# A hybrid RG-LRU / gated delta net encoder: the turns of rg_loop cut at another place, the delta net's chunk matrices made in dn_project

## What is computed

```python
def rglru_mixer(y, w_in, conv_w, conv_b, gate_w, gate_b, lam, w_out):
    xb, zb = jnp.split(y @ w_in, 2, axis=-1)          # 1024 -> 2048 + 2048
    xb = dwconv(xb, conv_w) + conv_b                  # 4 taps along time
    for d in range(2):
        gates = einsum("btnc,gncm->gbtnm", xh, gate_w[d]) + gate_b[d]   # blocks of 256
        r, i = sigmoid(gates[0]), sigmoid(gates[1])
        log_a = -RG_C * softplus(-lam[d]) * r
        a = exp(log_a); b = sqrt(-expm1(2.0 * log_a)) * (i * xf)
        h_d = linear_recurrence(a, b)                 # d = 1 runs backwards
    return ((h_0 + h_1) * silu(zb)) @ w_out

# gated delta net, per direction, head and chunk
decay = exp(where(incl, gc[:, None] - gc[None, :], -inf))    # gc = cumsum(g)
a_mat = where(strict, einsum(kb, k) * decay, 0.0)            # kb = k * beta
sol = triangular_solve(a_mat + eye, [v * beta, kb * exp(gc)])
qk = einsum(q, k) * decay
# then the chunks of a head in a row: state s, outputs o
```

## Time and profile before

| | us |
|---|---|
| median of 3 runs | 3242.26 |
| lowest, highest | 3238.85, 3243.62 |
| the profiled execution | 3243.82 |
| its span | 3242.1 |
| PE busy | 2779.4 (86%) |
| DVE, ACT, POOL busy | 1628.7, 1224.1, 1253.5 |

### The profile page before, as it was taken

The page is one execution under the profiler, slowest core; times in us unless marked ns, Lnnn a source line. Parts: engine busy times, 40 slices in busy tenths (PEclk is TensorE's granted clock), DMA queues, the critical chain, the costliest instruction groups (busy, mean ns, idle before and its releaser), DMA issues. The chain is left out here.

```text
span 3242.1 us, 53074 instructions
## 1 busy us (share of the span) xinstructions
PE 2779.4 (86%) x19211; PEld 2661.3 (82%) x19211; DVE 1628.7 (50%) x2351; ACT 1224.1 (38%) x1989; POOL 1253.5 (39%) x1183
## 2 busy tenths in 40 slices
PE   4799999993997299999997998999989999995993
PEld 2788888883995199999996898888989889885992
DVE  3266666664202334444443776776767677663003
ACT  2255555553103134334433344534444453432001
POOL 3333333331220122222221766665666666642220
PEclk8899999996998599999998999998999899997996
DMA  3111111112314023332232312032131313114214
GB/s 108 53 52 52 52 52 52 52 39 87 111 65 171 19 72 90 94 93 88 85 91 69 92 18 74 17 78 51 40 77 17 74 17 76 28 17 145 79 39 170
DMA packets 187727, 223.34 MB, mean 69 GB/s; under 512 B 50715, under 2 KB 157548, under 8 KB 185884
## 3 DMA queue, kind: packets, MB, share of 16 engines
q1 hardware_dynamic: 182940, 203.98, 21.7%
q10 hardware_dynamic: 4608, 17.04, 1.6%
HBM read 152.77 MB, written 68.23 MB: 68 GB/s over the span
## 5 line engine op out<-in xcount | busy, mean ns | idle before, releaser
L1634 ACT ACTIVATE zz<-ps 104x416 fp32r<-104x416 f32 x560 | 284.9, 517 | 446.4 <-PE ps L1496 445.3
L537 PE MATMUL ps<-dn_yhi,dn_whi 128*128 128x416 f32 (+1 forms) x1152 | 387.1, 336 | 16.4 <-POOL dn_wlo L521 16.4
L538 PE MATMUL ps<-dn_ylo,dn_whi 128*128 128x416 f32 (+1 forms) x1152 | 376.1, 326 | 0.0
L539 PE MATMUL ps<-dn_yhi,dn_wlo 128*128 128x416 f32 (+1 forms) x1152 | 375.1, 326 | 0.0
L1726 DVE TENSOR_TENSOR pp<-ps,level_mask 104x416 fp32r<-104x416 f32 x560 | 318.8, 586 | 100.1 <-PE ps L1496 97.7
L1498 PE MATMUL ps<-pp,zz 104*104 104x208 f32 x1440 | 266.1, 295 | 41.4 <-ACT zz L1634 31.9
L537 PE MATMUL ps<-rg_yhi,rg_whi 128*128 128x416 f32 (+1 forms) x768 | 251.9, 328 | 45.8 <-POOL rg_wlo L521 40.4
L538 PE MATMUL ps<-rg_ylo,rg_whi 128*128 128x416 f32 (+1 forms) x768 | 251.6, 328 | 0.0
L539 PE MATMUL ps<-rg_yhi,rg_wlo 128*128 128x416 f32 (+1 forms) x768 | 250.6, 326 | 0.0
L1498 PE MATMUL ps<-zz,pp 104*104 104x208 f32 x1440 | 247.9, 282 | 0.0
L1498 PEld LDWEIGHTS ps<-pp,zz 104*104 104x104 f32 x1440 | 184.4, 176 | 67.2 <-ACT zz L1634 34.8
(11 more groups left out here) (275 smaller groups left out, 7476.8 us busy)
## 6 DMA issues: line engine op xcount, KB each, us to landing
dn_raw<-in_dn_w_in SPq DMA_DIRECT2D x48, 512.0 KB, 3.9
qd<-rows_scratch SPq DMA_DIRECT2D x160, 104.0 KB, 3.1
rg_raw<-in_rg_w_in SPq DMA_DIRECT2D x32, 512.0 KB, 3.8
o_scratch<-a SPq DMA_DIRECT2D x16, 520.0 KB, 2.8
rgo_oraw<-o_scratch ACTq DMA_DIRECT2D x16, 520.0 KB, 4.3
n_y<-y_scratch SPq DMA_DIRECT2D x16, 520.0 KB, 6.5
n_h<-h_scratch SPq DMA_DIRECT2D x16, 520.0 KB, 12.6
qk_scratch<-p_qk SPq DMA_DIRECT2D x16, 520.0 KB, 3.1
```

What stands on the lines that cost most here:

```text
L537: e.matmul(o, whi, mhi[:, t0:t0 + tn], start=(first and k == 0), stop=False)
L538: e.matmul(o, whi, mlo[:, t0:t0 + tn], start=False, stop=False)
L539: ins = e.matmul(o, wlo, mhi[:, t0:t0 + tn], start=False, stop=(last and k == end))
L1634: e.activation(zz[:, b, :, :], ps[0:CH, 2 * b + 1, 0:m4], ACT.Copy).then_inc(zev.sem, 1)
```

## The change

It has three parts, and a row of counters (`ahead`, `gone`) that let a phase start with loads for which no turn stands.

**rg_loop.** A turn n now makes units X0, X1 of block n + 1, then the gates of block n (direction 1 first), then Z0, Z1 of block n. X0 and X1 of block 0 stand ahead of the loop; the last turn has none. DVE's taps for block n + 1 stand between parts of block n.

```diff
+        xtile, tile = S("xtile", 2), S("tile", 10, 3)
         gate_hi = S("gate_hi", 2)
...
+        DT = [(d, t) for d in (1, 0) for t in range(2)]
+        X0, X1, G0, G1, Z0, Z1 = range(6)
...
+            def turn(n, last):
+                gone = 2 if last else 0
+                for t in range(0 if last else 2):
+                    e.wait_ge(x_out.sem, x_out.at(n, 2 * t + 2))
+                    e.wait_ge(z_out.sem, z_out.at(n, 2 * t - 2))
+                    columns(n, X0 + t, xtile)
+                e.wait_ge(xlo_done.sem, xlo_done.at(n, 2))
+                for q in range(8):
+                    i, g, t = q // 4, q // 2 % 2, q % 2
+                    if q % 4 == 0:
+                        e.wait_ge(wt.split.sem, wt.split.at(n, G0 + i + 1 - gone))
+                    if q >= 2:
+                        e.wait_ge(gate_out.sem, gate_out.at(n, 2 * q - 2))
+                    elif last:
+                        e.wait_ge(z_out.sem, z_out.at(n, 2 * q - 2))
...
-                    project(e, ps, 3 * (q % 2), wt, [(d, g * 512 + i * 256 + t * P) for i in range(2)],
+                        e.wait_ge(x_out.sem, x_out.at(n + 1, 2 * q + 2))
+                    project(e, ps, 3 * (q % 2), wt, [(i, g * 512 + k * 256 + t * P) for k in range(2)],
                             conv).then_inc(tile.sem, 1)
+                for t in range(2):
+                    e.wait_ge(gate_out.sem, gate_out.at(n, 14 + 2 * t))
+                    columns(n, Z0 + t, tile, gone)
...
+                decay(0), decay(1)
+                if not last:
+                    high(n + 1, 0)
+                z(0)
+                decay(2), decay(3)
+                if not last:
+                    high(n + 1, 1)
                 for i, (d, t) in enumerate(DT):
                     e.wait_ge(u_done.sem, u_done.at(n, i + 1))
                     e.activation(u[:, d, t, :], u[:, d, t, :], ACT.Sqrt).then_inc(s_done.sem, 1)
+                z(1)
+
...
+                if not last:
+                    taps_in(n + 1)
+                    convolve(n + 1, 0)
+                rest(0)
+                if not last:
+                    convolve(n + 1, 1)
+                rest(1), rest(2)
+                z(0)
+                rest(3)
+                recur(0), recur(1)
+                z(1)
+                recur(2), recur(3)
```

```diff
+        RING = 5
+        ex = sb(s, "p_ex", [CH, NC, 2, 2, CH])
+        gm, nq_own = sb(s, "p_gm", [CH, 2, 2, 2, CH]), sb(s, "p_nq", [CH, RING - 2, 2, 2, 2, CH])
+        gcol, bcol = sb(s, "p_gcol", [CH, 2, NC, 2]), sb(s, "p_bcol", [CH, 2, NC, 2])
+        nq_rn = rn[0:CH].rearrange("p a t -> p (a t)")[:, 0:16 * CH] \
+            .rearrange("p (b d q r i) -> p b d q r i", b=2, d=2, q=2, r=2)
+        nq = [nq_rn[:, 0], nq_rn[:, 1]] + [nq_own[:, i] for i in range(RING - 2)]
+        raw = sq[0:CH].rearrange("p a t -> p (a t)").rearrange("p (k q i) -> p k q i", k=NC, q=2)
...
+            def load_decays(n):
+                e.wait_ge(nb_done.sem, nb_done.at(n, 0))
+                e.wait_ge(qkt_done.sem, qkt_done.at(n, 0))
+                hold(e, s.passed)
+                for d in range(2):
+                    for r in range(2):
+                        src = gc_rows[d][bass.ds(n * 2 + r, 1), :].rearrange("r (k i) -> (r k) i", i=CH)
+                        e.dma_start(ex[:, :, d, r, :], src.partition_broadcast(CH)).then_inc(ex_in.sem, 16)
 
             def store_qk(n, i):
...
+                load_decays(n)
                 load(n, 4), load(n, 5)
                 ahead(0)
                 store_qk(n, 0)
                 ahead(1)
                 store_qk(n, 1)
+                store_rows(n, krow_dram, krow.rearrange("c k m -> c (k m)").unsqueeze(1), 3, krow_out)
+                store_nq(n, 0, 1)
                 ahead(2)
-                store_rows(n, krow_dram, krow.rearrange("c k m -> c (k m)").unsqueeze(1), 3, krow_out)
+                store_nq(n, 2)
                 store_z(n, 0)
+                store_nq(n, 3, 4, 5)
+                ahead(3)
                 store_rows(n, vrow_dram, vrow.rearrange("c k r m -> c (k r m)").unsqueeze(1), 8, vrow_out)
-                ahead(3)
+                store_nq(n, 6, 7, 8, 9)
                 store_z(n, 1)
...
+                def differences(*chunks):
+
+                    for k in chunks:
...
+                        for d in range(2):
+                            for r in range(2):
+                                ins = e.tensor_scalar(ex[:, k, d, r, :], ex[:, k, d, r, :],
+                                                      gcol[:, d, step_of(k, d), r:r + 1], 0.0,
+                                                      ALU.subtract, ALU.min)
+                        ins.then_inc(diff.sem, 1)
+
...
+                def strengths(*chunks):
...
+                        for d in range(2):
+                            v = nq[k % RING][:, d, 0]
+                            ins = e.tensor_tensor(v, v, bcol[:, d, step_of(k, d), :].unsqueeze(2)
...
+                split(n, 2)
+                differences(0, 1, 2, 3, 4)
+                split(n, 3)
+                differences(5, 6, 7, 8, 9)
+                split(n, 4), split(n, 5)
+                strengths(0, 1, 2, 3)
+                if not last:
+                    split(n + 1, 0)
+                strengths(4, 5, 6, 7, 8, 9)
+                if not last:
+                    split(n + 1, 1)
```

PE makes the products beside units 4 and 5 and the transposes of v behind them; ACT and DVE:

```diff
+                def beside_third(k):
+                    if k in (0, 2, 4, 6):
+                        sums(n, k // 4, k % 4 == 2)
+
+                def beside_fourth(k):
+                    if k < 3:
+                        keys_by_tokens(n, k)
+                    elif k >= 4:
+                        products(n, k - 4)
+
+                def beside_fifth(k):
+                    if k < 6:
+                        products(n, k + 4)
+                    if k >= 3:
+                        values_by_tokens(n, k - 3)
...
+                copy_in(0), tanh(0), square(0), copy_in(1), tanh(1), square(1), copy_in(2)
                 inverse_norm(0)
-                copy_in(3), tanh(3)
                 inverse_norm(1)
+                keys_out(0), keys_out(1), keys_out(2)
+                decays(0, 1, 2, 3, 4)
+                copy_in(3)
+                decays(5, 6, 7, 8, 9)
+                products_out(0, 1)
+                tanh(2)
+                products_out(2, 3)
+                tanh(3)
                 z(0)
-                for q in range(8):
-                    turn_out(q)
+                products_out(4, 5, 6, 7)
+                values_out(0)
+                products_out(8)
+                values_out(1)
+                products_out(9)
+                values_out(2), values_out(3), values_out(4)
                 z(1)
...
+                def systems(*chunks):
+
+                    for k in chunks:
+                        b = k % 2
+                        e.wait_ge(raw_done.sem, raw_done.at(n, k + 1))
+                        if k == 0:
+                            e.wait_ge(normed.sem, normed.at(n, 2))
+                        if k >= 2:
+                            e.wait_ge(qkt_done.sem, qkt_done.at(n, k - 1))
+                        e.tensor_tensor(gm[:, b], raw[:, k].unsqueeze(1).to_broadcast([CH, 2, 2, CH]),
+                                        c["gram_mask"][:, :, :, :], ALU.mult).then_inc(gm_done.sem, 1)
+                        e.wait_ge(gm_done.sem, gm_done.at(n, k + 1))
+                        e.wait_ge(e_done.sem, e_done.at(n, k + 1))
+                        e.wait_ge(nq_out[k % RING].sem, nq_out[k % RING].at(n, 16 * (k // RING)))
+                        for q, done in enumerate((nb_done, qkt_done)):
+                            e.tensor_tensor(nq[k % RING][:, :, q],
+                                            gm[:, b, :, q, :].unsqueeze(2).to_broadcast([CH, 2, 2, CH]),
+                                            ex[:, k], ALU.mult).then_inc(done.sem, 1)
+
+                conv(0), silu_of(0), conv(1), silu_of(1), conv(2)
+                norm(0), norm(1)
+                systems(0)
+                conv(3)
+                systems(1)
+                silu_of(2)
+                systems(2)
+                silu_of(3)
+                z(0)
+                systems(3, 4, 5, 6, 7, 8, 9)
+                z(1)
```

```diff
+    LN_AT, EXP_AT, SCALE_AT, GATE_AT = [3, 4, 5, 6, 8], [3, 4, 5, 6, 8], [4, 5, 6, 7, 9], [5, 6, 7, 8, 9]
...
+            def load_systems(n, g):
+                if g >= NC:
+                    e.wait_ge(om.sem, om.at(n, g - NC + 1))
+                hold(e, s.passed)
+                for d in range(2):
+                    src = nq_dram.rearrange("n k c (d x) -> c n k d x", d=2)
+                    e.dma_start(nq[:, g % NC, d].rearrange("c q r i -> c (q r i)").unsqueeze(1),
+                                src[:, bass.ds(n * 2 + g // NC, 1), chunk(g, d), d, :]).then_inc(nq_in[g % NC].sem, 16)
...
-                    e.wait_ge(nb_done.sem, nb_done.at(n, g + 1))
```

(18 more changed lines are left out.)

738 lines of the change are left out of this document (392 added, 346 removed).

## The result

| | before | after |
|---|---|---|
| median | 3242.9 us | 3343.4 us |
| lowest, highest (4 runs each) | 3238.9, 3247.4 | 3330.5, 3345.7 |
| profiled execution, span | 3242.1 us | 3343.9 us |
| mean granted clock | 0.926 | 0.915 |

The ratio is 1.0302, with a 95% interval from 1.0277 to 1.0328: 98 us slower, and 100 between the medians. The forecast was 3318, in a range from 3205 to 3390.

The account below looks back on a forecast made before the run. PE was taken as the bound, with hardly any slack in dn_project (19 us). 3243.8 (profiled) - 8 (rg_loop) + 4 (dn_tables) + 200 (dn_project) - 120 (dn_chunks) = 3320, so about 3318 us as median; range 3205 to 3390.

Parts of the forecast that it names:

- main case: Whole kernel: the summed forecast of about 3318 us holds, within 3290 to 3350; chance 0.55.
- second rival: dn_project: POOL's differences cost 0.4 us or more, or waits lower PE's clock; head 109 to 112, 3360 to 3385; chance 0.15.
- Part two: dn_tables and dn_project: work moved in lengthens a head from 77.9 to 102.6 us; +200 us, plus 4 for dn_tables.
- Part one: rg_loop: the new turn order removes the gates' 5.9 us wait per block for POOL's xlo; -8 us, bounds -15 and +10.
- z's way out of PSUM: rg_loop: z0 and z1 leave PSUM late, so PE idles 3.6 and 4.6 us a turn in place of the xlo wait.
- unit 1 at 18.8: dn_project: unit 1's split waits behind chunk 9's betas, so it starts at 18.8 us instead of 11.8.
- unit 3 behind the decay rows and 20 differences: dn_project: unit 3's split waits for that load and those instructions; it starts at 48.6 us instead of 42.3.
- The exclusion: DVE instructions with two SBUF inputs and POOL instructions don't run side by side; one waits for the other.
- the sum of 85 us: dn_project: DVE's 41 and POOL's 43.5 us a head exclude each other, exceeding PE's 80.7 and bounding the head.
- Part three: dn_chunks: removed Gram products and differences gain 80 us, heads' ends 35, the start 5; -120 us, bounds -75 and -150.
- No exclusion: dn_project: first rival, DVE and POOL hardly delay each other; head 87.6 us, 3210 us in all; chance 0.20.
- rg_loop at 70.6 us a turn: rg_loop: third rival, z's rows leave in time and PE never idles; -65 in place of -8, 3262 us; chance 0.07.

Follow-up runs that it names:

- the kernels with the splits ahead: Changed kernel with GpSimd's splits of units 3 and 4 moved ahead of the differences: 3249.0 us; with betas also moved to dn_chunks: 3203.1 us.
- the best kernel: Changed kernel with differences on ACT, betas in dn_chunks, ACT's and DVE's queues reordered, next head's split held back, v1 and last values' copies made earlier: 3147.8 us.

## Why the prediction was right, and where it was not

**The direction and the size** were right: dn_project had no slack on PE, and it lost more than dn_chunks won. 3343 lies in the main case's own range (3290 to 3350), but in part by luck. The head of 109.3 to 112 us is the second rival's to the microsecond, and its reasons, dearer differences and half clock, are what the trace shows. Part two came out 43 us dearer than the sum had it, and 18 us that the sum had wrong elsewhere pull the time back: parts one and three gave 14 more (with the edge ahead of dn_chunks), and dn_tables' +4 is 0.7.

**Part one**, -8, is -10. A turn was to last 78.7 us and lasts 78.9 in most, without the wait for xlo. The wait that takes its place is the one that was named, z's way out of PSUM: 2.5 and 3.8 us a turn in most, where I had 3.6 and 4.6.

```profile
PE ps L543 <- DVE zs L829: 35.9, 12, 3.8
```

But the sum is near by luck. The terms that the text writes out, seven turns at -1 and +5 in the tail, come to -2 and not to -8, and two more were off and cancelled. PE's last matmul in rg_loop comes 7.7 us later, not earlier, since PE waits 8.2 us for a split in the first turn and 13.3 us in the last ahead of the gates. And the tail from there to the last output is 18.7 us, where I wrote 42 against 37: I had counted it from the last gate. In the new order two units of Z stand behind the gates, so that the roots and scans run beside them; before, nothing did (PE is busy for 0.1 of 53.4 us between its last matmul there and the next stage's first).

**Part two**, +200, is +243, at a head of 109.3 to 112 where 102.6 stood. Its two waits came out the other way round. The first, unit 1 at 18.8, fell away: it starts at 11.8. The step that failed is the price of a chunk's matrices and betas in turn, put at 3.2 us and 2.2 in the trace; the last ones end 7 us into the next head, not 14. The second, unit 3 behind the decay rows and 20 differences, was named right and sized wrong: 6.3 us forecast, 18.8 measured. The rows were asked for at 21, not 31, and came at 36.4, not 39. What failed is the price of a difference: 0.27, taken from a select of the same shape, with 0.40 as the upper bound; it is 0.63, and 0.73 in the mean. The 20 of them take 14.5 us instead of 5.4. The nearest row by shape was the wrong neighbour: a copy of these elements takes 0.27 us and this form 0.63, while twice the elements add 0.3. The prediction's estimate of 0.16 us for 104 elements is further off still: no form measured here takes less than 0.26. The two waits are not independent, either. When unit 3 starts is set by the rows and the differences alone: it starts at 54.3, 5.7 us later than the 48.6 of the forecast, and the 7 us that the first wait no longer takes only make the second longer. To that comes half clock in unit 3, 2.0 us, which I had put in the bounds only. In sum seven heads are 224 us longer (forecast 173) and the first 19 (12), and the 14 us of tail after the last head are not there: the edge to dn_chunks is 27.5 us, against 30.1 before.

**The exclusion** itself holds for what it was read from. The masked product p_gm, which read PSUM at 573 to 592 ns, has a median of 918 ns now:

```profile
L1502 DVE TENSOR_TENSOR p_gm<-p_sq,gram_mask x80: 579/918/1421, 1200.2 to 1996.8; 104x416 f32<-104x416 f32 x80
```

With betas gone from POOL it is 586 where the differences are still on POOL, and 584 where they are on ACT; with the differences on ACT and betas on POOL it stays at 918. So it is betas. But the sum of 85 us, which I called a bound, is none that decides: the kernels with the splits ahead show that what bound the head was the order in queues. The Trainium skill, page "SBUF — State Buffer", section "Who interferes with whom", states that a DVE instruction with two SBUF inputs contends with a GpSimd instruction that reads SBUF. These numbers agree with it, and so do the 6.65 and 3.97 us of the same three taps.

**Part three**, -120, is -129, or -132 with the edge ahead of it. PE's removed work gives 2.0 in a quiet period, as I took it, but nothing that shows at the heads' ends, so it is 59 us in all where I had 80. The quiet periods lose 2.4 each. The heads' ends, which I had halved, are better than half: 10 to 12 us over a quiet period before, 1 to 9 after.

**The rivals.** That POOL's differences cost 0.4 or more was true, and by it I had the head at 109 to 112, 3360 to 3385: right in the price and in the head, and 17 to 42 us too high in the time, since the tail of 14 us wasn't there and part three gave 12 more. No exclusion, and rg_loop at 70.6 us a turn, did not happen.

## What to carry to other kernels

Before work is moved onto an engine that has room, look at what stands behind it in that engine's queue: 20 instructions of 0.63 us ahead of a split cost 18.8 us of PE a head, and the same 20 behind it 6. Work that waits for a transfer never goes ahead of work that somebody else waits for, and where one engine frees PSUM banks, its long jobs are cut and laid between the short copies. A price is taken from the same form of instruction, not only from the same shape.

## What the runs showed of the hardware

GpSimd's tensor_scalar on 104x104 floats takes 0.54 us with one operation, 0.63 with two, against 0.27 for a copy; ACT makes the same difference (relu with a column as bias) in 0.37 (median of 320), and DVE in 0.26 to 0.37. The four loads that spread a row over 104 partitions take SP 8.3 us to issue, where a weight load takes 0.4. In the best kernel PE waits 2 us at the end of each head, and in every second head the granted clock then falls to 0.50, 1.2 in place of 2.4 GHz, although PE has been at work again for 2 us; that head is 84.4 us long, the others 82.8. The window is of PE's first unit there, columns as above:

```profile
1464.50:1466.50 2.00, 2.00 (x8) 1.91 (x8) 1.97 (x5) 1.91 (x5) 0.00 (x0) 0.50 0.64 211
```

Why it is every second head and not each stays open.
